# Decoder layer with an expert FFN: a raw buffer for each weight tile of a gate block, the three gate tiles ahead, and the early dot products in two stages instead of three

## The reference

```python
proj = einsum('bsd,de->bse', h, w_in)          # heads' columns | 3 x 1024 gate columns
a_out, b_out, c_out = dilated attention, gated recurrence, memory attention   # 512 wide each
branches = stack([a_out, b_out, c_out], axis=2)
gates = sigmoid((gate_logits + b_gate).reshape(b, s, 3, D))
widened = einsum('bsgw,gwd->bsgd', branches, w_branch)
merged = sum(gates * widened, axis=2)
mix = einsum('bsd,de->bse', merged, w_out)
h = layer_norm(ALPHA * h + mix)
# PEER, 128 experts a token, chosen by two top-16 searches over h @ w_peer_q:
act = gelu(einsum('td,ted->te', xt, u_tab[it]))
h = layer_norm(ALPHA * h + einsum('te,ted->td', gate * act, v_tab[it]))
```

## Time and profile before

| | us |
|---|---|
| median of three runs | 4232.38 (4225.43 to 4239.48) |
| the profiled execution | 4228.72, span 4226.6 |
| TensorE busy | 3707.9 (88% of the span) |
| VectorE busy | 2705.7 (64%) |
| GpSimdE busy | 1550.9 (37%) |
| ScalarE busy | 1368.2 (32%) |
| gated stage, half 0 and half 1 | 545 to 770, and 1462 to 1696 |
| query stage, half 0 and half 1 | 846 to 940, and 1794 to 1898 |

### The profile page before, as it was taken

The page is one execution under the profiler, slowest core; times in us unless marked ns, Lnnn a source line. Parts: engine busy times, 40 slices in busy tenths (PEclk is TensorE's granted clock), DMA queues, the critical chain, the costliest instruction groups (busy, mean ns, idle before and its releaser), DMA issues.

```text
span 4226.6 us, 46191 instructions
## 1 busy us (share of the span) xinstructions
PE 3707.9 (88%) x14431; PEld 2459.3 (58%) x14431; DVE 2705.7 (64%) x5477; ACT 1368.2 (32%) x2741; POOL 1550.9 (37%) x1317
## 2 busy tenths in 40 slices
PE   7999989899888799687437989799799999999998
PEld 5777867678777677475113445354354545545763
DVE  1444443307776765649899988988886878842550
ACT  1444443223434433126024042141240513314540
POOL 2555534230000176465455344443454444420000
PEclk8999999899999999796869999899899999999999
DMA  7667623355444377688999999999999999973557
GB/s 242 199 203 228 206 70 90 96 184 161 142 137 141 91 239 240 233 299 303 374 337 408 384 375 376 350 404 368 352 400 403 404 403 405 396 302 127 182 197 275
DMA packets 505249, 1133.37 MB, mean 268 GB/s; under 512 B 37932, under 2 KB 250076, under 8 KB 504832
## 3 DMA queue, kind: packets, MB, share of 16 engines
q1 hardware_dynamic: 336512, 570.42, 39.2%
q0 software_dynamic: 147456, 536.94, 33.3%
q10 hardware_dynamic: 21120, 24.12, 1.6%
HBM read 1044.28 MB, written 89.41 MB: 268 GB/s over the span
## 4 chain that ended last, share of the span: by engine, by line
PE 34%; DVE 13%; DMA 5%; issue 3%; ACT 1%; POOL 0%; DVEq 0%; ACTq 0%
PE ps L1277 26%; DVE u_ring L2212 6%; PE ps L1263 4%; DMA u_ring<-in_peer_u,pidx 4%; PE ps L1310 3%; DMA v_ring<-in_peer_v 1%; DVE hot L2204 1%; DVE hot L2205 1%; DVE split_v L2259 1%; ACT split_v L1688 0%; DVE pick_own L1843 0%; DVE pick_own L1848 0%; DVE got_own L1851 0%; PE h_up L1252 0%; DVE inds_own L1794 0%
## 5 line engine op out<-in xcount | busy, mean ns | idle before, releaser
L1277 PE MATMUL ps<-v_ring,table 128*128 128x512 f32 x3584 | 1595.0, 596 | 22.4 <-DMA v_ring<-in_peer_v 21.2
L899 POOL DMA_INDIRECT u_ring<-in_peer_u,pidx x896 | 861.5, 961 | 1005.1 <-DVE coefe L2212 921.2
L2212 DVE CUSTOM_DVE_ANT_0 u_ring<-u_ring,h_up 128x1024 f32<-128x1024 f32 x896 | 1061.3, 1217 | 157.2 <-DMA u_ring<-in_peer_u,pidx 145.7
L1277 PEld LDWEIGHTS ps<-v_ring,table 128*128 128x128 f32 x3584 | 664.4, 191 | 779.3 <-issue 727.3
L848 POOL TENSOR_TENSOR w_lo<-w_raw,w_hi 128x1024 fp32r<-128x1024 f32 x200 | 442.1, 2216 | 881.3 <-ACT w_hi L1383 875.7
L958 PE MATMUL ps<-x_hi,w_hi 128*128 128x512 f32 x1280 | 525.4, 410 | 68.7 <-ACT w_hi L1383 59.6
L961 PE MATMUL ps<-x_lo,w_hi 128*128 128x512 f32 x1280 | 511.8, 400 | 0.0
L1263 PEld LDWEIGHTS ps<-hot,hot 128*128 128x128 f32 x2048 | 281.1, 203 | 186.3 <-issue 104.9
L1656 ACT ACTIVATE table<-ps 128x512 f32<-128x512 f32 (+3 forms) x256 | 228.9, 894 | 426.4 <-PE ps L1263 370.4
L1644 ACT ACTIVATE hot<-hot,by_slot 128x128 f32<-128x128 f32 x1024 | 321.3, 387 | 111.3 <-DVE hot L2204 99.6
L1263 PE MATMUL ps<-hot,hot 128*128 128x128 f32 x2048 | 293.3, 289 | 61.4 <-DVE hot L2205 38.3
(11 more groups left out here) (294 smaller groups left out, 4077.5 us busy)
## 6 DMA issues: line engine op xcount, KB each, us to landing
v_ring<-in_peer_v SPq DMA_DIRECT2D x576, 512.0 KB
w_raw<-in_w_in SPq DMA_DIRECT2D x104, 512.0 KB
wh_d<-w_hi SPq DMA_DIRECT2D x56, 512.0 KB, 2.7
wl_d<-w_lo SPq DMA_DIRECT2D x56, 512.0 KB, 4.2
w_hi<-wh_d SPq DMA_DIRECT2D x56, 512.0 KB, 3.7
w_lo<-wl_d SPq DMA_DIRECT2D x56, 512.0 KB, 3.7
w_raw<-in_w_peer_q SPq DMA_DIRECT2D x32, 512.0 KB
u_ring<-in_peer_u,pidx POOLq DMA_INDIRECT x896
```

The costliest lines, as they stand in the source:

```text
L899: pool.indirect_dma_start(out=u_ring[:, slot_of(n, k), :], out_offset=None, in_=u_tab, in_offset=bass.IndirectOffsetOnAxis(ap=pidx[n % 2][ ...
L1277: last = pe.matmul(ps[2 * (n % 2) + c][:, :], table[:, row_of(n, i1), :], v_ring[:, j % V_TILES, HALF * c:HALF * c + HALF], start=(n == p ...
L2212: dve.tensor_tensor_reduce(out=u_ring[:, slot_of(n, k), :], in0=u_ring[:, slot_of(n, k), :], in1=h1_up[:, :, :].rearrange("p c n -> p (c n)"),
```

## The change

Each tile of a column block gets a raw buffer of its own, the order becomes G0 G1 G2 B0 B1 B2, each of the six results has a PSUM bank, and loads go up to a block ahead (tiles G2, B0, B1, B2 in `raw_mid`; in half 1 that lies where the heads' tables were, so SyncE loads it behind the barrier). G0 and G1 of the first block are computed before the barrier that ends the heads. The query stage gets two more raw buffers. The loop over blocks starts at 1 on all engines but GpSimdE and VectorE. Of the early dot products, 12 instead of 8 go to each column block, from its third tile on, and none to the query stage; the copied indices have three places instead of two.

```diff
-E_MID, E_OUT, E_PQ = 8, 8, 8
+E_MID, E_OUT = 12, 8
+MID_K = [D // P] * 3 + [4] * 3
-        MP = Steps(sem("mid_pe"), "G0 B0 G1 B1 G2 B2".split())
+        MP = Steps(sem("mid_pe"), "G0 G1 G2 B0 B1 B2".split())
+        def mid_raw(hf, j, t):
+            if t < 2:
+                return w_raw[t], w_landed[t], 16 * (first_raw(hf) + j) + 16
+            return raw_mid[hf][t - 2], raw_in[t - 2], 16 * (KD * hf + j) + 16
 ...
-            def weight(b, m, src, k=KD):
-                sp.wait_ge(w_split[b], 2 * m + 2)
+            def weight(b, m, raw, src, behind, k=KD):
+                buf, landed, _ = raw
+                sp.wait_ge(w_split[b], 2 * (m - behind) + 4)
 ...
                     for t in range(NT_MID):
-                        split_lo_only(t % 2, t0 + T_MID // 2 + NT_MID // 2 * j + t // 2, KD if t % 2 == 0 else NH)
-                        if hf == 1:
-                            u_rows(E_MID * t // NT_MID, E_MID * (t + 1) // NT_MID, E_MID // E_ROWS * j, E_MID * j)
+                        split_lo_only(t % 2, t0 + T_MID // 2 + NT_MID // 2 * j + t // 2, mid_raw(hf, j, t)[0], MID_K[t])
+                        if hf == 1 and t >= 2:
+                            u_rows(E_MID * (t - 2) // 4, E_MID * (t - 1) // 4, E_MID // E_ROWS * j, E_MID * j)
 ...
                     for t in range(4):
-                        split_lo_only(t % 2, t0 + T_PQ // 2 + 2 * e + t // 2)
-                        if hf == 1:
-                            u_rows(E_PQ * t // 4, E_PQ * (t + 1) // 4, G_PQ + E_PQ // E_ROWS * e, E_ROWS * G_PQ + E_PQ * e)
+                        split_lo_only(t % 2, t0 + T_PQ // 2 + 2 * e + t // 2, pq_raw(hf, e, t // 2, t % 2)[0])
 ...
+                def gated(j, t):
+                    it = KD * hf + j
+                    b = t % 3
+                    n = (t % 2, t0 + T_MID // 2 + NT_MID // 2 * j + t // 2)
+                    if t < 3:
+                        pe.wait_ge(MA.sem, MA.after(f"s{b}", it - 1))
+                        last = tile(n, x_hi, x_lo, KD, ps[b][:, :])
+                    else:
+                        pe.wait_ge(MV.sem, MV.after(f"g{b}", it - 1))
+                        pe.wait_ge(o_split, 6 * hf + 2 * b + 2)
+                        last = tile(n, o_hi[...], o_lo[...], NH, ps[3 + b][:, :])
+                pe.wait_ge(V.sem, V.after("vt2", NH * hf + NH - 1))
+                gated(0, 0)
+                pe.wait_ge(AC.sem, AC.after("q2", NH * hf + NH - 1))
+                gated(0, 1)
                 cross(pe, boundary(hf, 1))
 ...
+                def mid_gates(j):
+                    for b in range(3):
+                        act.activation(sgate[:, b, :], ps[b][:, :], ACT.Sigmoid, ...)
+                        mid_hi(j, 3 + b)
+                for t in range(2):
+                    mid_hi(0, t)
+                cross(act, boundary(hf, 1))
+                mid_hi(0, 2)
+                mid_gates(0)
+                with act.Fori(1, KD) as j:
+                    for t in range(3):
+                        mid_hi(j, t)
+                    mid_gates(j)
 ...
                     for b in range(3):
                         if hf == 1:
-                            e_rows(2 * b, 2 * b + 2, E_MID // E_ROWS * j, E_MID * j)
+                            e_rows(E_MID * b // 4, E_MID * (b + 1) // 4, E_MID // E_ROWS * j, E_MID * j)
 ...
                 cross(dve, boundary(hf, 3))
                 if hf == 1:
-                    with dve.Fori(0, PH // 2) as e:
-                        e_rows(0, E_PQ, G_PQ + E_PQ // E_ROWS * e, E_ROWS * G_PQ + E_PQ * e)
                     e_gates()
```

More of the change, by code:

```diff
@@ L385, in layer, with raw_at @@
         coef = coefe
+        def raw_at(name, offset, k):
+            return nc.alloc_sbuf_tensor_at(name, [P, k, P], F32, offset=offset)
+        assert where["state"] + 12 * NH * P <= where["w_raw0"] and where["causal"] + 4 * KD * P <= where["cols"]
+        raw_mid = [[raw_at(f"raw_mid{hf}_{t}", o, MID_K[t]) for t, o in zip(range(2, NT_MID), offsets)] for hf, offsets in enumerate((
+            [r_side + 2048 * i for i in (0, 2, 3, 4)],
+            [where["causal"]] + [where["state"] + 2048 * i for i in range(3)]))]
+        raw_pq = [raw_at(f"raw_pq{b}", r_top + 4 * NB * D + 4096 * b, KD) for b in range(2)]
+        assert r_top + 4 * NB * D + 8192 <= where["m_hi"]
         split_v = [[nc.alloc_sbuf_tensor_at(f"split_v{part}_{i}", [P, D], F32R, offset=where["u_ring"] + (2 * i + part) * D * 4)
@@ L433, in layer @@
         w_landed = [sem(f"w_landed{i}") for i in range(2)]
+        raw_in = [sem(f"raw_in{t}") for t in range(2, NT_MID)]
+        raw_pq_in = [sem(f"raw_pq_in{b}") for b in range(2)]
         w_split = [sem(f"w_split{i}") for i in range(2)]
@@ L723, in late_weights @@
                     for t in range(2):
-                        weight(t, skip + T_OUT // 2 + e, w_out[:, :, 2 * P * e + P * t:2 * P * e + P * t + P])
-                with sp.Fori(0, PH) as e:
+                        weight(t, LATER * hf + T_OUT // 2 + e, out_raw(hf, e, t), w_out[:, :, 2 * P * e + P * t:2 * P * e + P * t + P], 1 if e else 3)
+                for e in range(PH):
                     for t in range(2):
-                        weight(t, skip + T_PQ // 2 + e, w_pq[:, :, bass.ds(2 * P * e + P * t, P)])
+                        weight(t, LATER * hf + T_PQ // 2 + e, pq_raw(hf, e // 2, e % 2, t),
+                               w_pq[:, :, 2 * P * e + P * t:2 * P * e + P * t + P], 2 if e else 1)
             def first_half():
@@ L741, in first_half @@
                     save(n)
-                with sp.Fori(0, KD) as j:
+                for t in range(NT_MID):
+                    mid_weight(0, 0, t, 1 if t < 2 else 3)
+                with sp.Fori(1, KD) as j:
                     for t in range(NT_MID):
-                        mid_weight(0, j, t)
-                late_weights(0, 0)
+                        mid_weight(0, j, t, 3)
+                late_weights(0)
             def second_half():
@@ L1614, in query, with query_hi @@
                     act.dma_start(qp_d[hf, bass.ds(2 * e + t, 1)].rearrange("a p k -> (a p) k"), qst[t][:, :]).then_inc(qp_out[t], 16)
-                weight_hi(0, t0 + T_PQ // 2)
-                weight_hi(1, t0 + T_PQ // 2)
+                def query_hi(e, t):
+                    weight_hi(t, t0 + T_PQ // 2 + e, pq_raw(hf, e // 2, e % 2, t))
+                query_hi(0, 0)
+                query_hi(0, 1)
                 query(0, 0)
-                with act.Fori(1, PH) as e:
-                    weight_hi(0, t0 + T_PQ // 2 + e)
+                for e in range(1, PH):
+                    query_hi(e, 0)
                     query(e - 1, 1)
-                    weight_hi(1, t0 + T_PQ // 2 + e)
+                    query_hi(e, 1)
                     query(e, 0)
```

92 lines of the change are left out of this document (46 added, 46 removed).

## The result

The changed kernel takes 4266.13 us (median of 5 executions, 4261.32 to 4275.32), the kernel before 4229.61 (median of 5, 4225.43 to 4239.48). The ratio is 1.0087, with a 95% interval from 1.0071 to 1.0103: 36.5 us slower, where 23 were forecast. The time lies in the forecast range (4230 to 4269), near its slow end and beyond the narrower 4243 to 4261 that the prediction gave 0.47, and the sign is right. The profiled execution of the changed kernel was its slowest, 4275.32 us with a span of 4273.5.

What follows compares the result with a forecast made beforehand. TensorE set the pace before; GpSimdE was to become the bound in half 1's gated stage. 45.2 us lost there, less 14.4 (half 0) and 7.9 (query stage), made 22.9 slower: 4252 us, range 4230 to 4269.

Steps and rivals of the forecast that it cites:

- Half 0, blocks 1 to 7: Gated stage of half 0: both TensorE holes in each block close, 7 x 1.68 = 11.8 us gained.
- The edge of half 0: From heads to gates in half 0: TensorE starts 3.2 us earlier, 2.6 us gained by block 1 (1 to 3.2).
- its second and third part come about 0.7 us late each: Half 0's edge: VectorE's splitting of branch outputs takes 13.9 us, its later parts reaching B1 and B2 about 0.7 us late.
- The query stage: Query stage of half 1: without 32 gathers and with earlier loads it takes half 0's time, 7.9 us gained.
- either cure: Query stage of half 1: taking out its 32 gathers, or loading weights two tiles ahead; together 7.9 us gained.
- Half 1, the bound: Gated stage of half 1: GpSimdE becomes the bound, 28.9 us of own work a block, 32.3 with waits.
- Block 0: Start of half 1's gated stage: TensorE waits for G2's weights, block 1 begins late, 13.7 us lost (8.7 to 16).
- The end: End of half 1's gated stage: projection starts 39.3 us after the last block's beginning, against 35.1; 4.2 us lost.
- as before: Output projection of half 1: SyncE, ScalarE and the projection's 32 dot products were claimed unchanged.
- the ring: Half 1's gated stage: four gather slots; gather k+4 is issued only when dot product k is done, making GpSimdE wait.
- the first: Rival for half 1: the ring never binds, gathers land in under 4.9 us, 30.0 us a block, 4231 us; chance 0.24.
- The third: Rival: slower memory and clock, gathers land in 6.7 us, 34.5 us a block in half 1, 4269 us; chance 0.17.

Runs made afterwards that it cites:

- e4_edges: The changed kernel with SyncE's two gate loads behind the head loop again and TensorE's first two gate tiles behind the barrier again: 4243.07 us, ratio 1.0043.
- e2_before12: The kernel before with only the dot products placed as in the change (12 a column block, none in the query stage): 4239.92 us, ratio 1.0033.
- the second profile of the kernel before: The kernel before run and profiled once more, nothing changed: 4226.41 us in one execution.
- e5_match: e4_edges with two gathers behind each of a block's six low parts and VectorE's dot products reordered, six ahead of the first gate product: 4227.59 us, ratio 0.9997.
- e7_early8: e1_dots8 with the edits of e4_edges, and a block's gathers and dot products moved to its beginning: 4195.15 us, ratio 0.9916.
- e1_dots8: The changed kernel with dot products spread 8, 8, 8 over the three stages again, query stage included: 4208.52 us, ratio 0.9959.

## Why the prediction was right, and where it missed

**Half 0, blocks 1 to 7:** 11.8 us forecast. The period went from 26.16 to 24.48 us, no hole is left, and seven periods take 171.6 us where before took 184.4, 12.8 us less. Right.

**The edge of half 0:** 2.6 us gained by block 1 were forecast, 2.3 were lost (587.64 against 585.32, the first matmul of block 1), the largest miss in half 0. The first steps held: start 553.5 (553.7 forecast), G2 at 568.7 (568.0), a hole of 1.4 us (1.6). The step that failed is "its second and third part come about 0.7 us late each". The second did (0.71), the third came 2.53 us late, since the split took 15.9 us instead of 13.9, and the matmuls behind that hole ran 0.43 us apart instead of 0.23, at 1.2 GHz (granted clock 0.50 from 583.3 to 586.5), which the sum had left out there. The start 3.2 us earlier came from the missing table load and the early high part, as the sum had it. What it did not weigh is the two tiles ahead of the barrier by themselves: they are worth 0.35 us of that start (e4_edges) and cost the stage 7.6 us.

**The stretch between the halves:** 3.0 us lost, nothing forecast. The prediction never listed where SyncE's two gate loads went: from behind the head loop to ahead of it, past the load of the queries. With them behind it again the stretch is 5.9 us shorter; the kernel before and e2_before12 took 16.1 to 18.0 there.

**The query stage:** 7.25 and 0.6 us forecast, 7.25 and 0.17 measured. That the stage comes down to half 0's 81.6 us held in every kernel with either cure; that the gain measured 7.25 is luck in part, since it goes by the same profile as the forecast, and the second profile of the kernel before (84.13) leaves 2.5. The reason held only half: each of the two cures gives all of it.

**Half 1, the bound:** GpSimdE's own work, 28.9 us, is the block of e2_before12 (29.2) and e5_match (28.8). With waits 32.3 us were forecast, 32.16 measured; TensorE stands 3.2 us in B2 where some 4 were forecast. **Block 0:** from the start of the stage to block 1, 34.1 us before and 48.6 after, 14.5 lost for 13.7; TensorE waited 5.42 us for G2's weights, where the sum had some 5.2. **The end:** 37.75 us from the last block's beginning, against 39.3 forecast and 35.1 before. Together 43.6 us for 45.2, by the first profile of the kernel before; by the second 52.1.

**The output projection:** "as before" was the step, 4.6 us the miss; some 2 of it go with the new buffers and order and the rest with the 12 dot products, by the runs above.

Edge, stretch and output projection make 4.9 + 3.0 + 4.6 = 12.5 of the 13.6 us by which the change is slower than forecast, by the same single profiles; the terms that came out well, half 1's above all, are sure only to the scatter of 8.5 us named above. The mechanism of half 1 was right, and the range was wide enough for three costs that were put at nothing or as a gain. **The rivals:** the ring binds, and a gather is used 5.4 us after its issue where the first needed under 4.9, so the first is out. The third named nearly the right time, 4269, for wrong reasons: no block of 1 to 7 takes 34.5 us. But it also took the edge of half 0 at 1 us instead of 2.6, and stood nearer there.

## What to carry to other kernels

Work that fills gaps should stay in the stage where the engine that issues it has room once the rest of the change is made: the query stage had room for all 32 gathers as soon as its weights came early. Here a ring between two queues bound by the order of both: when tiles are reordered on one engine, reorder the producer and the consumer of the ring together. A tile pulled ahead of a barrier holds everything behind the barrier for its whole length.

## What the runs showed of the hardware

An addition of two SBUF tiles on VectorE, 0.69 us alone, takes up to 4.9 us when it falls beside two wide low parts of GpSimdE in a row (4.75 to 4.90 in blocks 0 to 6 of half 1, in the changed kernel). It ends 0.56 us behind them (1540.59, the end of the first row of the block shown above):

```profile
1536.25 4.90 DVE L2164 TENSOR_TENSOR macc<-macc 128x512 f32<-128x512 f32 x1
```

The group of these additions from 1500 to 1734 us in the changed kernel, and in e5_match (from 1490 to 1690), where the two never meet:

```profile
L2164 DVE TENSOR_TENSOR macc<-macc 128x512 f32<-128x512 f32 x15 | 45.7, 3046 | 0.5
```

```profile
L2164 DVE TENSOR_TENSOR macc<-macc 128x512 f32<-128x512 f32 x14 | 9.7, 692 | 0.5
```

The Trainium skill, page SBUF — State Buffer, section SBUF: two separate sides, calls the port pair of VectorE and GpSimdE an exclusive lock for the whole instruction, and names additions with both inputs in SBUF among those that want it. The trace agrees with a lock and not with a shared rate, and it shows more: the addition came during the first low part and did not get in between the two. The 4.9 us stood off TensorE's path in the changed kernel, since the gathers issued next do not wait beyond their index copy; no run prices the held additions alone.

The other way round it is seen at the stage's edge: in e7_early8 two gathers took 2.45 and 2.70 us while VectorE split the branches, against 0.94 to 0.98 for most others. And a high DMA share was no sign of a bound here: the query stage of e1_dots8 runs at the matmuls' pace (81.60 us, as half 0's) with the DMA engines busy 98% of it.
